# An encoder layer in split float32: the normalised input starts at 64 modulo 256 bytes, and its plain products run in two halves of 256 tokens

## Chip, cores and metric

One core of one Trainium2 chip runs the whole kernel. The metric is device time in microseconds (us), lower is better; three runs were timed.

## The reference

Input `x` is 512 tokens by 1024 features, float32. One layer is computed, and a final RMS norm:

```python
x = x + 0.5 * swiglu(rms_norm(x, ffn1_norm), ffn1_gate, ffn1_up, ffn1_down)   # 1024 -> 2816 -> 1024
x = x + hybrid_mixer(rms_norm(x, mix_norm), w_in, ...)    # w_in 1024 x 3088, w_out 1024 x 1024
x = x + 0.5 * swiglu(rms_norm(x, ffn2_norm), ffn2_gate, ffn2_up, ffn2_down)
return rms_norm(x, final_norm)

def swiglu(h, w_gate, w_up, w_down):
    return (jax.nn.silu(h @ w_gate) * (h @ w_up)) @ w_down
```

The mixer projects the normalised input with `w_in` into the queries, keys, values and gates of a gated linear attention (4 heads, chunks of 64), of a differential attention (4 heads, blocks of 128 queries) and of a short convolution, runs the three, joins their outputs and multiplies them by `w_out`.

## The kernel before

**Precision and layout.** Activations lie transposed in SBUF: features on the 128 partitions, 512 tokens along the free axis, 8 tiles of features. Every large product is made of three matmuls (`three`, lines 519 to 523): each operand is split into a high and a low part in `F32R`, and high x high, high x low and low x high are added up in PSUM. ScalarE makes the high part (`split_hi`, line 1033, for weights), VectorE the low one (`split_lo`, line 1409). `xg_hi` and `xg_lo` hold the normalised input's two parts (before the division by the root mean square, which is applied to the outputs).

**Addresses.** `sb(name, shape)` gives out SBUF in order; tensors opened on one nested stack share memory with those of the next stack. Behind `xg_hi` and `xg_lo` (16384 bytes each on a partition) come `w_hi` and `w_lo` (9216 each), then a region that holds `h` (45056) and, behind a pad of 48 floats (192 bytes), `s_hi` and `s_lo`. Sizes but the pads are multiples of 256. `sum_hi` and `sum_lo` lie behind one more pad of 64 bytes, so that they, the weights' parts `w_hi`, `w_lo`, `h` and `h_hi` start at the same place modulo 256 as `xg` does. Each slice that a matmul takes of `xg` or `s` begins a multiple of 1024 bytes from its tensor's start.

**Order of work.** Up and gate products of FFN 1, its down product, the mixer (27 slabs of `w_in`), `w_out`, then FFN 2 the same way as FFN 1. A slab is 8 blocks of 128 x 128 weights; SP loads it into one of two slots of `raw`, ScalarE and VectorE split it into one of two slots of `w_hi`, `w_lo`, and TensorE waits for it (`wait_slab`).

- *Plain tiles.* The first `PLAIN` = 4 of the 22 tiles of an FFN's hidden features are computed plainly, a gate and an up product each (`pair`, `product`): 8 blocks, three matmuls of 512 columns per block, with `xg` streamed. The very first pair (`first_pair`) does both products block by block while the data arrive.
- *Fast units.* The other `FAST` = 18 tiles use Winograd's form of Strassen's scheme on 2 x 2 blocks: seven block products in place of eight. A unit has 84 matmuls of 256 columns. m1, its companion and m4 stream halves of `xg` (`x_block`; 36 matmuls); m3, m5, m6 and m7 stream sums of activations `s_hi`, `s_lo` (`s_block`; 48). The weights' sums are made by GpSimd (`sums`, lines 445 to 456), split by ScalarE (`ga`, `gb`, line 1152) and VectorE (lines 1465, 1470, 1475) into `sum_hi`, `sum_lo`. ScalarE copies partial results out of PSUM into `snap` (`take`, line 1128), VectorE combines them: lines 1520, 1488, 1525, 1494, 1502 and 1482 (`c11`, `c21`, scaling, `c12`, `gated`, `c22`). ScalarE's own order in a unit is `snap[2]`, `gb`, `split_hi`, `snap[0]`, SiLU of the unit before (line 1134, after line 1488), the `sum_hi` of line 1152, `snap[1]`, `ga`. TensorE's m7 waits for `snap[1]` (lines 663 to 665); VectorE's line 1482 waits for `snap[2]`, which is m7's result.
- *Mixer.* The list `MIX` has 18 transposed tiles ("T": weights loaded, `xg` streamed, 512 columns) and 9 slabs of natural tiles ("N": `xg` loaded as the stationary operand, `w_hi`, `w_lo` streamed, 384 columns). Between the work of a slab, twice per slab, `side(hook(j, half))` puts in the small matmuls of attention and of the recurrence.
- *Last tile.* The last output tile of FFN 2 (`last_tile`) is done in two halves of 256 tokens, with its weights split into the memory of `xg` (`last_hi`, `last_lo`).

Of the kernel before, what the change touches and what calls it, by code (L numbers as in the profile page):

```python
# [29 lines left out]
P = 128  # L30
# [3 lines left out]
KT = D // P  # L34
# [56 lines left out]
def hook(j, half):  # L91
    return 2 * j + half
# [35 lines left out]
def half_tokens(c):  # L128
    return slice(c * HALF, (c + 1) * HALF)
# [25 lines left out]
def build_layer(nc, xT, up_w, down_w, t_w, nat_w, out_w, gains, gk_up, gk_bias, gla_gain, diff_gain,  # L155
                lam_qk, rel_bias, conv_w, onehot, decay_mats, level_masks, ident_c, out):
    tvec = nc.dram_tensor("bias_by_distance", (HEADS * COPIES, 5 * P), F32, kind="Internal")
    with ExitStack() as ctx:
        def sb(name, shape, dt=F32, stack=ctx):
            return stack.enter_context(nc.sbuf_tensor(name, shape, dt))  # L160
# [2 lines left out]
            return ctx.enter_context(nc.semaphore(name))  # L163


        xg_hi = sb("xg_hi", [P, KT, S], F32R)
        xg_lo = sb("xg_lo", [P, KT, S], F32R)
        w_hi = sb("w_hi", [P, 2, SLOTW], F32R)
        w_lo = sb("w_lo", [P, 2, SLOTW], F32R)

# [81 lines left out]
        ps = ctx.enter_context(nc.psum_tensor("ps", [P, 8, S], F32))  # L252
# [262 lines left out]
        def _(pe):  # L515
            def wait_slab(s, n=0):
                pe.wait_ge(lo_ready, n + (s + 1))
# [7 lines left out]
            def part(s, lo, hi):  # L525
                return w_hi[:, slot(s), lo:hi], w_lo[:, slot(s), lo:hi]
# [24 lines left out]
            def spread_rms(phase):  # L551

                pe.wait_ge(diag_ready, phase + 1)
                for b in range(NB):
                    last = pe.matmul(ps[:, STAT, b * P:(b + 1) * P], ones[:], rinv[:, b * P:(b + 1) * P],
                                     start=True, stop=True)
                last.then_inc(stat_ready, 1)
# [15 lines left out]
                        if k == KT - 1:  # L573
                            last.then_inc(slab_used, 1)

            def product(s, bank, first_use, n=0, spread_at=None):
                wait_slab(s, n)
                for k in range(KT):
                    if k == spread_at:
                        spread_rms(0)  # L580
                    if first_use is not None:
                        pe.wait_ge(xg_lo_ready, first_use + k + 1)
                    last = three(ps[:, bank, :], part(s, k * P, (k + 1) * P), (xg_hi[:, k, :], xg_lo[:, k, :]),
                                 k == 0, k == KT - 1)
                return last

            def ffn_up(f, up0):
                phase = 2 * f

                def pair(m):  # L590
                    b = m % 2
                    first = m == 0
                    if m + f >= 2:
                        pe.wait_ge(gate_scaled, PLAIN * f + m - 1)
                        pe.wait_ge(h_ready, FT * f + m - 1)
                    g = up0 + 2 * m
                    last = product(g, b, KT * phase if first else None)
                    last.then_inc(slab_used, 1)
                    second = m == 1 and phase == 0
                    if second or (first and phase):  # L600
                        mean_squares(phase)
                    last = product(g + 1, 2 + b, None, spread_at=KT // 2 if second else None)
                    last.then_inc(slab_used, 1)
                    if first:
                        spread_rms(phase)
# [346 lines left out]
            for j, kind in enumerate(MIX):  # L952
# [4 lines left out]
                if kind[0] == "T":  # L957
# [2 lines left out]
                        pe.wait_ge(tile_copied, t - 1)  # L960
                    if n_nat:
                        pe.wait_ge(nat_copied, NB * (n_nat - 1) + t % 2 + 1)
                    for k in range(KT):
                        last = three(ps[:, t % 2, :], part(s, k * P, (k + 1) * P), (xg_hi[:, k, :], xg_lo[:, k, :]),
                                     k == 0, k == KT - 1)
                        if k == KT // 2 - 1:
                            side(hook(j, 0))
                    last.then_inc(slab_used, 1)

                else:  # L970
                    _, sec, k0, nk = kind
# [1064 lines left out]
```

## Time and profile before

| what | value |
|---|---|
| median of 3 runs | 989.5 us (989.37 to 989.78) |
| profiled execution, own time | 989.01 us |
| its span, first to last instruction | 987.2 us |
| mean granted TensorE clock | 0.994 |
| TensorE busy | 964.1 us (98%) |
| VectorE busy | 682.4 us (69%) |
| ScalarE busy | 437.7 us (44%) |
| GpSimd busy | 353.2 us (36%) |
| read from HBM | 92.00 MB |

The profile is of one execution. A matmul's record covers more than the time in which it keeps the next one back, so the rate is read from starts and not from durations. A clock of 1.00 is the full one. In the rows, PE is TensorE, DVE is VectorE, ACT is ScalarE, POOL is GpSimd; `ps<-a,b` is a matmul with `a` streamed and `b` loaded; square brackets at the end of a row give the idle time of the engine before it and what released it.

### The profile page before, as it was taken

The numbers are of one execution on the slowest core, as the hardware profiler recorded it, in microseconds if no ns is written. First come the engines' busy times: TensorE is split into PE (matmuls) and PEld (weight loads), VectorE is DVE, ScalarE is ACT, GpSimd is POOL, SyncE is SP. The second block draws the span as 40 slices with busy tenths as digits, with TensorE's granted clock in tenths as the row PEclk, the third lists the DMA queues.
The fourth block names the chain that finished last, engine by engine and source line by source line (L and its number), as shares of the span: only waits on it lengthen the run. The fifth ranks groups of instructions, "written<-read, shape, count | busy, mean of one in ns | idle before, by whom it ended". The sixth has DMA issues, their size and how long they took to land.

```text
span 987.2 us, 16662 instructions
## 1 busy us (share of the span) xinstructions
PE 964.1 (98%) x6362; PEld 859.4 (87%) x6362; DVE 682.4 (69%) x948; ACT 437.7 (44%) x687; POOL 353.2 (36%) x229
## 2 busy tenths in 40 slices
PE   9999999999999999999989999999999999999997
PEld 7789999998888888777978788888999999888887
DVE  6599999987534364775756874459999999753444
ACT  7555454555422223555723233355545454542331
POOL 0766767670012151000102004367776767000001
PEclk9999999999999999999979999999999999999999
DMA  6323232322222244112211123233333332222322
GB/s 203 135 81 117 94 124 88 127 85 93 90 87 96 96 133 135 65 47 66 74 39 65 55 74 107 85 107 107 105 109 110 102 115 97 64 96 96 97 96 86
DMA packets 30639, 95.07 MB, mean 96 GB/s; under 512 B 4113, under 2 KB 7345, under 8 KB 30593
## 3 DMA queue, kind: packets, MB, share of 16 engines
q1 hardware_dynamic: 29264, 91.77, 28.4%
q0 software_dynamic: 896, 2.39, 0.8%
q8 instruction: 31, 0.51, 0.2%
q10 hardware_dynamic: 432, 0.28, 0.1%
q14 instruction: 16, 0.12, 0.0%
HBM read 92.00 MB, written 2.42 MB: 96 GB/s over the span
## 4 chain that ended last, share of the span: by engine, by line
PE 42%; DVE 5%; ACT 2%; issue 1%; POOL 0%; DVEq 0%; POOLq 0%; ACTq 0%
PE ps L521 13%; PE ps L523 13%; PE ps L522 13%; ACT w_hi L1033 1%; DVE w_lo L1409 1%; DVE s_lo L1460 1%; DVE e_dec L1742 1%; PE ps L861 1%; DVE a_comp L1762 1%; ACT h L1041 0%; PE ps L893 0%; PE ps L901 0%; PE ps L831 0%; DVE states L1788 0%; DVE h_lo L1556 0%
## 5 line engine op out<-in xcount | busy, mean ns | idle before, releaser
L1409 DVE TENSOR_TENSOR w_lo<-raw,w_hi 128x1024 fp32r<-128x1024 f32 (+3 forms) x130 | 191.6, 1474 | 167.4 <-ACT w_hi L1033 167.3
L1033 ACT ACTIVATE w_hi<-raw 128x1024 fp32r<-128x1024 f32 (+3 forms) x130 | 134.2, 1032 | 209.2 <-PE ps L523 208.7
L521 PE MATMUL ps<-xg_hi,w_hi 128*128 128x256 f32 (+1 forms) x552 | 188.1, 341 | 4.0 <-DVE w_lo L1409 2.4
L523 PE MATMUL ps<-xg_hi,w_lo 128*128 128x256 f32 (+1 forms) x552 | 184.4, 334 | 0.0
L522 PE MATMUL ps<-xg_lo,w_hi 128*128 128x256 f32 (+1 forms) x552 | 184.2, 334 | 0.0
L521 PE MATMUL ps<-s_hi,sum_hi 128*128 128x256 f32 x576 | 159.7, 277 | 1.8 <-ACT snap L1128 1.7
L522 PE MATMUL ps<-s_lo,sum_hi 128*128 128x256 f32 x576 | 159.3, 276 | 0.0
L523 PE MATMUL ps<-s_hi,sum_lo 128*128 128x256 f32 x576 | 159.1, 276 | 0.0
L522 PE MATMUL ps<-h_lo,w_hi 128*128 128x512 f32 x330 | 128.4, 389 | 0.0
L521 PEld LDWEIGHTS ps<-xg_hi,w_hi 128*128 128x128 f32 x552 | 104.4, 189 | 24.1 <-issue 13.4
L523 PEld LDWEIGHTS ps<-xg_hi,w_lo 128*128 128x128 f32 x552 | 104.4, 189 | 10.8
L522 PEld LDWEIGHTS ps<-xg_lo,w_hi 128*128 128x128 f32 x552 | 104.5, 189 | 9.3
L521 PEld LDWEIGHTS ps<-s_hi,sum_hi 128*128 128x128 f32 x576 | 108.3, 188 | 2.5 <-issue 2.5
L522 PEld LDWEIGHTS ps<-s_lo,sum_hi 128*128 128x128 f32 x576 | 108.3, 188 | 0.0
L523 PEld LDWEIGHTS ps<-s_hi,sum_lo 128*128 128x128 f32 x576 | 108.2, 188 | 0.0
L521 PE MATMUL ps<-h_hi_s,w_hi 128*128 128x512 f32 x240 | 93.6, 390 | 0.6 <-DVE h_lo L1556 0.6
L523 PE MATMUL ps<-h_hi_s,w_lo 128*128 128x512 f32 x240 | 93.4, 389 | 0.0
L445 POOL TENSOR_TENSOR t_raw<-raw,raw_u 128x512 f32<-128x512 f32 x36 | 56.0, 1554 | 84.6 <-DMA raw_u<-up_w 74.8
L449 POOL TENSOR_TENSOR t_raw<-raw_u 128x512 f32<-128x512 f32 x36 | 76.4, 2122 | 0.0
L456 POOL TENSOR_TENSOR raw_u<-t_raw,raw 128x512 f32<-128x512 f32 x36 | 70.3, 1953 | 14.4 <-DVE w_lo L1409 7.1
L1134 ACT ACTIVATE gate_s<-gate_s 128x512 f32<-128x512 f32 x34 | 21.5, 634 | 117.6 <-DVE gate_s L1488 117.6
L522 PEld LDWEIGHTS ps<-h_lo,w_hi 128*128 128x128 f32 x330 | 62.0, 188 | 12.5
(243 smaller groups left out, 1901.2 us busy)
## 6 DMA issues: line engine op xcount, KB each, us to landing
raw<-up_w SPq DMA_DIRECT2D x50, 512.0 KB, 4.2
raw<-down_w SPq DMA_DIRECT2D x38, 512.0 KB, 3.3
raw_u<-up_w SPq DMA_DIRECT2D x36, 512.0 KB, 3.3
raw<-t_w SPq DMA_DIRECT2D x18, 512.0 KB, 3.2
raw<-out_w SPq DMA_DIRECT2D x8, 512.0 KB, 3.3
raw<-nat_w SPq DMA_DIRECT2D x6, 576.0 KB, 3.9
x<-xT SPq DMA_DIRECT2D x8, 256.0 KB, 5.3
out<-x SPq DMA_DIRECT2D x8, 256.0 KB, 2.2
```

The lines of the kernel that those rows point to most:

```text
L445: pool.tensor_tensor(t_raw[:, T1, :], raw[:, slot(s), 0:HW], raw_u[:, b, 0:HW], ALU.add)\
L449: pool.tensor_tensor(t_raw[:, T3, :], raw_u[:, b, 0:HW], raw_u[:, b, HW:UPW], ALU.add)\
L456: pool.tensor_tensor(raw_u[:, b, 0:HW], t_raw[:, T2, :], raw[:, slot(s), HW:UPW], ALU.add)\
L521: pe.matmul(out_ap, a[0], b[0], start=first, stop=False, skip_group_check=resumed)
L522: pe.matmul(out_ap, a[0], b[1], start=False, stop=False, skip_group_check=resumed)
L523: return pe.matmul(out_ap, a[1], b[0], start=False, stop=last, skip_group_check=resumed)
L861: last = pe.matmul(ps[c * CHUNK:(c + 1) * CHUNK, bank + hd, col + b * CHUNK:col + (b + 1) * CHUNK], a, bb, start=True, stop=True)
L1033: act.activation(dst, raw[:, slot(s), 0:w], ACT.Copy).then_inc(hi_ready, 1)
L1134: act.activation(gate_s[:, b, :], gate_s[:, b, :], ACT.Silu).then_inc(silu_done, 1)
L1409: dve.tensor_tensor(lo, raw[:, slot(s), 0:w], hi, ALU.subtract).then_inc(lo_ready, 1)
L1460: dve.tensor_tensor(s_lo[:, j, :, :], s_raw[:, j, :, :], s_hi[:, j, :, :], ALU.subtract)\
L1742: dve.tensor_tensor(e, e, g, ALU.mult).then_inc(products_ready, 1)
```

## The change

Two pads, of 192 bytes below `xg_hi` and of 320 above `xg_lo`, move `xg` by 192 bytes and everything behind it by 512. The plain products and the transposed tiles of the mixer are computed in two halves of 256 tokens, all eight blocks for the first half and then all eight for the second; what stood between the fourth and the fifth block (`spread_rms`, the hook) stands between the halves. The gate product of FFN 2's first pair, `first_pair` and the natural tiles keep their shape.

```diff
--- before.py
+++ after.py
@@ -163,8 +163,10 @@
             return ctx.enter_context(nc.semaphore(name))
 
 
+        sb("below_xg", [P, 48])
         xg_hi = sb("xg_hi", [P, KT, S], F32R)
         xg_lo = sb("xg_lo", [P, KT, S], F32R)
+        sb("above_xg", [P, 80])
         w_hi = sb("w_hi", [P, 2, SLOTW], F32R)
         w_lo = sb("w_lo", [P, 2, SLOTW], F32R)
 
@@ -573,15 +575,24 @@
                         if k == KT - 1:
                             last.then_inc(slab_used, 1)
 
-            def product(s, bank, first_use, n=0, spread_at=None):
-                wait_slab(s, n)
+            def product(s, bank, first_use):
+                wait_slab(s)
                 for k in range(KT):
-                    if k == spread_at:
-                        spread_rms(0)
-                    if first_use is not None:
-                        pe.wait_ge(xg_lo_ready, first_use + k + 1)
+                    pe.wait_ge(xg_lo_ready, first_use + k + 1)
                     last = three(ps[:, bank, :], part(s, k * P, (k + 1) * P), (xg_hi[:, k, :], xg_lo[:, k, :]),
                                  k == 0, k == KT - 1)
+                return last
+
+            def product_by_halves(s, bank, between):
+
+                wait_slab(s)
+                for c in range(2):
+                    t = half_tokens(c)
+                    for k in range(KT):
+                        last = three(ps[:, bank, t], part(s, k * P, (k + 1) * P), (xg_hi[:, k, t], xg_lo[:, k, t]),
+                                     k == 0, k == KT - 1)
+                    if c == 0 and between is not None:
+                        between()
                 return last
 
             def ffn_up(f, up0):
@@ -594,12 +605,15 @@
                         pe.wait_ge(gate_scaled, PLAIN * f + m - 1)
                         pe.wait_ge(h_ready, FT * f + m - 1)
                     g = up0 + 2 * m
-                    last = product(g, b, KT * phase if first else None)
+                    if first:
+                        last = product(g, b, KT * phase)
+                    else:
+                        last = product_by_halves(g, b, None)
                     last.then_inc(slab_used, 1)
                     second = m == 1 and phase == 0
                     if second or (first and phase):
                         mean_squares(phase)
-                    last = product(g + 1, 2 + b, None, spread_at=KT // 2 if second else None)
+                    last = product_by_halves(g + 1, 2 + b, (lambda: spread_rms(0)) if second else None)
                     last.then_inc(slab_used, 1)
                     if first:
                         spread_rms(phase)
@@ -960,12 +974,7 @@
                         pe.wait_ge(tile_copied, t - 1)
                     if n_nat:
                         pe.wait_ge(nat_copied, NB * (n_nat - 1) + t % 2 + 1)
-                    for k in range(KT):
-                        last = three(ps[:, t % 2, :], part(s, k * P, (k + 1) * P), (xg_hi[:, k, :], xg_lo[:, k, :]),
-                                     k == 0, k == KT - 1)
-                        if k == KT // 2 - 1:
-                            side(hook(j, 0))
-                    last.then_inc(slab_used, 1)
+                    product_by_halves(s, t % 2, lambda: side(hook(j, 0))).then_inc(slab_used, 1)
 
                 else:
                     _, sec, k0, nk = kind
```

## Rows read from the trace of the kernel before

**Rows 1.** the page, busy time, share of the span and instructions of each engine
```profile
PE 964.1 (98%) x6362; PEld 859.4 (87%) x6362; DVE 682.4 (69%) x948; ACT 437.7 (44%) x687; POOL 353.2 (36%) x229
```

**Rows 2.** TensorE's groups by shape: line, streamed and loaded operand, count; busy, mean ns
```profile
L521 PE MATMUL ps<-s_hi,sum_hi 128*128 128x256 f32 x576 | 159.7, 277 | 1.8 <-ACT snap L1128 1.7
...
L521 PE MATMUL ps<-xg_hi,w_hi 128*128 128x512 f32 x264 | 106.6, 404 | 1.9 <-ACT dv L1360 0.8 <-issue 0.7 <-DVE w_lo L1409 0.3
...
L521 PE MATMUL ps<-xg_hi,w_hi 128*128 128x256 f32 x288 | 81.5, 283 | 2.1 <-DVE w_lo L1409 2.1
...
L521 PE MATMUL ps<-xg_hi,sum_hi 128*128 128x256 f32 x144 | 40.9, 284 | 1.1 <-ACT snap L1128 1.1
...
L521 PE MATMUL ps<-w_hi,xg_hi 128*128 128x384 f32 x96 | 33.4, 348 | 0.0
...
L522 PE MATMUL ps<-h_lo,xg_hi 128*128 128x256 f32 x44 | 12.4, 283 | 0.0
```

**Rows 3.** timeline of TensorE, one steady unit: start us, duration us
```profile
752.71 0.28 PE L521 MATMUL ps<-xg_hi,w_hi 128*128 128x256 f32 x1
...
757.01 0.29 PE L521 MATMUL ps<-s_hi,sum_hi 128*128 128x256 f32 x1
...
761.11 0.28 PE L521 MATMUL ps<-s_hi,sum_hi 128*128 128x256 f32 x1
...
762.47 0.28 PE L521 MATMUL ps<-xg_hi,w_hi 128*128 128x256 f32 x1
```

**Rows 4.** ten steady units: window, busy us (instructions) of each engine, granted clock, DMA
```profile
713.67:811.27 97.60, 97.60 (x843) 97.60 (x841) 91.20 (x101) 50.65 (x80) 70.97 (x41) 1.00 0.33 107
```

**Rows 5.** timeline of TensorE, 512 columns: steady, and behind a hook
```profile
20.12 0.39 PE L523 MATMUL ps<-xg_hi,w_lo 128*128 128x512 f32 x1
...
20.80 0.39 PE L523 MATMUL ps<-xg_hi,w_lo 128*128 128x512 f32 x1
...
430.54 0.50 PE L521 MATMUL ps<-xg_hi,w_hi 128*128 128x512 f32 x1
...
433.39 0.27 PE L796 MATMUL ps<-ident,u 128*128 128x128 f32 x1
```

**Rows 6.** timeline of VectorE, steady units
```profile
734.17 0.41 DVE L1482 SCALAR_TENSOR_TENSOR h<-ps,snap 128x256 f32 x1
...
753.54 0.43 DVE L1482 SCALAR_TENSOR_TENSOR h<-ps,snap 128x256 f32 x1
...
755.62 2.32 DVE L1409 TENSOR_TENSOR w_lo<-raw,w_hi 128x1024 fp32r<-128x1024 f32 x1
...
758.20 0.41 DVE L1488 TENSOR_TENSOR gate_s<-ps,rinv 128x256 f32<-128x256 f32 x1
...
760.32 1.30 DVE L1475 TENSOR_TENSOR sum_lo<-raw_u,sum_hi 128x1024 fp32r<-128x1024 f32 x1 [0.61 <-ACT sum_hi L1152]
...
763.24 0.41 DVE L1482 SCALAR_TENSOR_TENSOR h<-ps,snap 128x256 f32 x1
```

**Rows 7.** timeline of ScalarE in the same unit
```profile
758.70 0.63 ACT L1134 ACTIVATE gate_s<-gate_s 128x512 f32<-128x512 f32 x1 [3.59 <-DVE gate_s L1488]
...
760.18 0.36 ACT L1128 ACTIVATE snap<-ps 128x256 f32<-128x256 f32 x1
```

**Rows 8.** timeline of TensorE, m7 of the third unit of FFN 1
```profile
84.27 0.36 PE L521 MATMUL ps<-s_hi,sum_hi 128*128 128x256 f32 x1 [0.99 <-ACT snap L1128]
```

**Rows 9.** timeline of GpSimd in the unit of rows 6
```profile
755.50 1.35 POOL L445 TENSOR_TENSOR t_raw<-raw,raw_u 128x512 f32<-128x512 f32 x1 [2.44 <-DMA raw_u<-up_w]
```

**Rows 10.** timeline of VectorE in two late units of FFN 1
```profile
205.69 1.21 DVE L1409 TENSOR_TENSOR w_lo<-raw,w_hi 128x1024 fp32r<-128x1024 f32 x1
...
208.82 0.42 DVE L1494 SCALAR_TENSOR_TENSOR h<-ps,snap 128x256 f32 x1 [0.49 <-PE ps L523]
...
215.51 1.21 DVE L1409 TENSOR_TENSOR w_lo<-raw,w_hi 128x1024 fp32r<-128x1024 f32 x1
```

**Rows 11.** VectorE writing s_lo: count, ns min/median/max, first and last start
```profile
L1460 DVE TENSOR_TENSOR s_lo<-h,s_hi x8: 1212/2310/2318, 46.4 to 671.9; 128x1024 fp32r<-128x1024 f32 x8
```

## The prediction

> **What bounds the kernel now.** I read the page first: TensorE is busy for 98% of the span [rows 1]. Then the groups of matmuls by shape, which give the counts [rows 2]. The durations there hold a tail that overlaps the next matmul, so the price of a matmul is the distance between two starts, read from TensorE's timeline. In one unit of the fast loop, the 36 matmuls that stream `xg` start at 752.71 and end where `s` takes over at 757.01: 4.30 us, 119.4 ns each (120 once settled). The last 12 that stream `s`, 761.11 to 762.47, take 113.3 ns each [rows 3]. Both are 256 columns against weights of the same kind, at the full granted clock, 2.4 GHz [rows 4], where 256 columns alone are 106.7 ns. With `xg` it is 120 in the groups against `w` and against `sum` alike, 283 ns in duration where `s` has 277 [rows 2]. What differs is the start: between `xg` and `s` the allocations are multiples of 256 bytes, but for a pad of 192, so `s` lies at 64 modulo 256 and `xg` at 128. With 512 columns at 128, three matmuls take 0.68 us, 226.7 ns each, against 213.3 of columns alone [rows 5]. So at 128 a matmul carries 13.3 ns on top whatever its width, and at 64, with 256 columns, 6.7.
>
> Then VectorE's timeline of the same unit, since it is busy for 91.2 of 97.6 us there [rows 4]. This decides the forecast. Its cycle, from one `h` of line 1482 to the next, is 9.70 us (753.54 to 763.24) with no wait for TensorE in it, against TensorE's 9.76 (752.71 to 762.47) [rows 3, 6]. Its one idle spell, 0.61 us before line 1475, is a wait for ScalarE, and ScalarE had waited for VectorE's line 1488 [rows 6, 7]. The chain is closed: 1488 at 758.20, SiLU at 758.70, `sum_hi`, then the copy of `snap` at 760.18 that ends at 760.54, and `sum_lo`. TensorE's product m7 needs that `snap` and starts at 761.11, 0.57 us after it [rows 3]. At 84.27, where the steady part of the first fast loop begins, m7 started right behind `snap` after 0.99 us of idle time [rows 8]; the same shows at 702.45 for the second FFN. So both loops start with TensorE waiting for VectorE, and the lead VectorE then gains is small.
>
> **The change, part by part.**
>
> *The offset.* `xg_hi` and `xg_lo` move to 64 modulo 256; all else keeps its place modulo 256. A unit's 36 `xg` matmuls fall from 4.30 to 36 x 0.1133 = 4.08 us, and the `s` part loses some 0.02 of settling, so TensorE's own unit falls by 0.24, from 9.76 to 84 x 0.1133 = 9.52. With TensorE alone, 36 units would give 8.6 us. But VectorE's cycle is 9.70, of which TensorE's speed changes nothing: the lengths that stretch it come from GpSimd's work (line 1409 takes 2.32 us while GpSimd's line 445 runs [rows 6, 9], and 1.21 where VectorE came first [rows 10]). From the anchor at 84.27 to m7 of the last unit are 15 units: 15 x (9.76 - 9.69) = 1.05 us, with 9.69 the mean of the three free cycles from 734.17 to 763.24 [rows 6]. Some cycles differ: VectorE starts line 1409 just before GpSimd, ends it 1.1 us sooner, and then waits 0.49 us for TensorE at line 1494; from 205.69 to 215.51 is 9.82 with that wait [rows 10]. I count five such cycles in the 30. A faster TensorE takes the wait away, which leaves 9.33, 0.36 under the free cycle, though some of it comes back as contention. Half of 2.5 x 0.36 is 0.4, rounded down to 0.35. That makes 1.4 us for each loop, **2.8** for both. Bounds: 0.5 for each if VectorE's cycle only eats the end's slack, 15 x 0.24 = 3.6 if it doesn't bind at all; so 1.0 to 7.2. The units before the anchors give nothing, as TensorE idles behind ScalarE and VectorE there.
>
> *The halves.* Of the 768 matmuls of 512 columns in plain products (six in the first FFN after the first pair, eight in the second) and in 18 transposed tiles, 24 each, the gate product of the second FFN's first pair stays whole. That leaves 744, which become 1488 of 256 columns with their weights loaded twice. 1488 x 113.3 = 168.6 us against 744 x 226.7 = 168.7: **0**. This rests on the price of `s` holding for `xg` against `w_hi` and `w_lo`. Those lie where `sum_hi` and `sum_lo` lie modulo 256, and today `xg` costs 120 against both, which speaks for it. If they cost 120 after all, the halves cost 744 x 13.3 = 9.9 us more; that is a rival. Loading 256 columns' weights keeps pace in the `s` parts. Line by line, the work between the halves (attention, transposes, scores) stands where it stood, halfway through a tile, and no wait is added. The consumers wait for the tile's last matmul, as before.
>
> The Trainium skill (TensorE: Matmul & The Clock Gate, Back-to-back issue gap) gives N / 2.4 + 2.5 ns, which is 109.2 ns for 256 columns wherever the operand lies. By it the offset would save nothing and each split would cost 2.5 ns, 1.9 us in all. The trace shows two prices for one width, so here it does not hold as it stands.
>
> *The settling after a hook.* After the small matmuls between halves, 12 matmuls of 512 columns take 2.85 us (430.54 to 433.39) against 2.72 in a steady run [rows 5]: 0.13 more. The first weight load after the hook stays exposed; with 256 columns I take 0.015 less for the settling behind it. With two such places in each of 18 tiles, 36 x 0.015 = **0.5** us gained; bounds 0 and 36 x 0.13 = 4.7, the low end being the nearer.
>
> *512 columns at 64.* The first pair of slabs (48 matmuls) and the gate product above (24) stay whole with `xg` at 64, for which no row exists. Below: 213.3 + 6.7 = 220.0, 72 x 6.7 = 0.5 us gained. Above: the extra doubles to 26.7, 72 x 13.3 = 1.0 lost. I take **0**.
>
> *`xg` as the stationary operand.* In the natural tiles (96 x 3 = 288 matmuls of 384 columns [rows 2]) `xg` is what is loaded, and in the last output tile (44 x 3 = 132 of 256 columns [rows 2]) weights lie in its memory. If what counts is the distance between the two operands, each gains or loses 6.7 ns: 1.9 and 0.9 us, either way. If only the streamed operand counts, nothing. I take **0**; the natural tiles' share is partly behind waits anyway.
>
> *ScalarE, VectorE, DMA.* They write and read `xg` at 64 now. No cost: VectorE writes `s_lo` at 64 in 1.21 us at best [rows 11], the 1.21 of `w_lo` at 128 [rows 10].  Instruction count rises by 744 matmuls and their loads on TensorE's queue; the straight-line last tile already runs 256-column matmuls without gaps.
>
> Sum: 2.8 + 0 + 0.5 + 0 + 0 = 3.3 us. The profiled execution took 989.0 us (span 987.2 and 1.8 around it); 989.0 - 3.3 = 985.7. The median of the runs is 0.5 above it, which gives **986.2**.
>
> **Rivals.**
>
> 1. VectorE gives way, TensorE keeps its 9.52. For it: the cycles of [rows 10], where VectorE waits; GpSimd was ahead of line 1409 by only 0.12 us (755.50 against 755.62 [rows 6, 9]), so the order may flip for good once VectorE never waits for TensorE. Against: in the free cycles it does not flip, and total contention per unit is much the same. 7.2 + 0.5 = 7.7 saved: 981.8. Chance 0.20.
>
> 2. Hidden or given back: the loops gain only 2.0 and the unpriced operands (512 at 64, `xg` loaded from 64) take it back: 2.0 - 1.0 - 1.0 = 0, so 989.5. For it: none of the three has a row. Chance 0.17.
>
> 3. Slower: the address is not what makes `s` cheaper. Then all splits pay the fixed 13.3 ns twice, 9.9 us, and nothing is gained: 999. It decides from 3.3 / 1488 = 2.2 ns more for each half matmul than 113.3. For it: no 256-column `xg` matmul at 64 is in the trace. Against: equal shapes, weights and clock in [rows 3]. Chance 0.08, a milder form included, in which the halves reach 116 to 118 and the loops gain nothing (4 to 7 us, 993 to 997). The Trainium skill's formula, above, would be another mild form, at 1.9 us.
>
> The forecast, VectorE's cycle setting the loops at 9.6 to 9.7, 984 to 988, has 0.55.
>
> **How the numbers follow.** This kernel's measurement tells about 0.2% (2 us) from no change, so faster means under 987.5. The forecast gives that in 0.8 of its cases (0.44), rival 1 always (0.20), rival 2 rarely (0.03): 0.67. Slower than 991.5: rival 3 and a small part of rival 2, 0.10. The rest, 0.23, lies between. The range reaches down past rival 1 with a little of the loaded operand's gain, 980.5, and up to rival 2 with 0.3 on top, 989.8; outside are the slower cases and a few lucky ones. The forecast's own range is 984 to 988.
>
> **What would show it.** In the profile after: starts of `xg` matmuls of 256 columns 113.3 ns apart in units, plain products and tiles (1, 3); the unit's length, 9.6 to 9.7 for me, 9.52 for rival 1, 9.76 for rival 3; idle time of TensorE before m7, released by ScalarE's `snap`, some 0.1 to 0.2 us in each unit, and no waits of VectorE at line 1494; the starts in the natural tiles (173.3 now) and in the last tile (120 now); the first pair's distance (226.7 now). I am wrong if VectorE's cycle falls below 9.5, if halves don't reach 113.3, or if 512 columns at 64 cost far more than the bounds.

## The result: slower by 0.36%

The changed kernel takes 993.2 us (median of 6 executions, 992.26 to 995.18) against 989.64 of the kernel before (6, 988.66 to 990.69): ratio 1.0036, 95% interval 1.0025 to 1.0046. I had forecast 986.2, with 980.5 to 989.8 as the range; the time is 3.4 us above that range. Line numbers differ between the kernels: in rows of the changed kernel and its variants the matmul helper is L523 to L525 (L521 to L523 before), `w_lo` L1418 (L1409), `snap` L1137 (L1128), and `c22`, the last write of `h` in a unit, L1491 (L1482).

The page of the changed kernel, busy time of the engines, answers to [rows 1]. TensorE has 744 more matmuls and is busy 4.4 us longer; the other engines' counts are as they were.

```profile
PE 968.5 (98%) x7106; PEld 896.5 (91%) x7106; DVE 684.3 (69%) x948; ACT 436.6 (44%) x687; POOL 357.8 (36%) x229
```

TensorE's groups by shape, against [rows 2]. I had read the gap between 277 (`s`) and 283 (`xg`) as two prices, and expected `xg` to come down to `s`. Both groups now stand at 281: `s`, which the change does not touch, came up.

```profile
L523 PE MATMUL ps<-s_hi,sum_hi 128*128 128x256 f32 x576 | 161.9, 281 | 1.8 <-ACT snap L1137 1.8
...
L523 PE MATMUL ps<-xg_hi,sum_hi 128*128 128x256 f32 x144 | 40.5, 281 | 1.1 <-ACT snap L1137 1.1
```

TensorE's timeline of one steady unit, against [rows 3] (start, duration):

```profile
745.10 0.28 PE L523 MATMUL ps<-xg_hi,w_hi 128*128 128x256 f32 x1
...
749.34 0.28 PE L523 MATMUL ps<-s_hi,sum_hi 128*128 128x256 f32 x1
...
753.58 0.28 PE L523 MATMUL ps<-s_hi,sum_hi 128*128 128x256 f32 x1
...
754.99 0.28 PE L523 MATMUL ps<-xg_hi,w_hi 128*128 128x256 f32 x1
```

The 36 `xg` matmuls take 4.24 us, 117.8 ns each, and the last 12 of `s` 1.41, 117.5 by these rounded starts. The unit is 9.89 us (84 x 117.8) where it was 9.76 and I wanted 9.52 to 9.69. From m7 of the third unit to m7 of the last, the first FFN's loop grew by 1.75 us and the second's by 1.53. These two make 3.28 us, and the whole span grew by 3.25 (987.22 to 990.47). The rest cancels. The first pair starts 0.74 us sooner, and the plain products of the second FFN gain 0.67. The transposed tiles up to the attention lose 0.50. One tile (541.29) loses 1.34 to the clock; of the fifteen profiles of this study nine have this tile slow and six have not, kernels with whole and with split products among either. The windows of that tile in the changed kernel and in the one before; the third number from the end is the granted clock (0.65 against 1.00, so that part of it ran at the 1.2 GHz level):

```profile
541.29:545.50 4.21, 4.21 (x26) 4.21 (x25) 2.70 (x4) 0.00 (x0) 0.00 (x0) 0.65 0.01 4
```

```profile
539.91:542.78 2.87, 2.87 (x16) 2.31 (x13) 2.63 (x4) 0.00 (x0) 0.00 (x0) 1.00 0.00 0
```

**Where 117.8 comes from.** 117.8 is not a fixed price: in the same trace, the steady part of the first loop starts at 113.3. TensorE's timeline around m7 of its fourth unit:

```profile
93.18 0.28 PE L523 MATMUL ps<-s_hi,sum_hi 128*128 128x256 f32 x1
93.30 0.28 PE L524 MATMUL ps<-s_lo,sum_hi 128*128 128x256 f32 x1
93.41 0.28 PE L525 MATMUL ps<-s_hi,sum_lo 128*128 128x256 f32 x1
93.56 0.36 PE L523 MATMUL ps<-s_hi,sum_hi 128*128 128x256 f32 x1
93.75 0.28 PE L524 MATMUL ps<-s_lo,sum_hi 128*128 128x256 f32 x1
93.87 0.28 PE L525 MATMUL ps<-s_hi,sum_lo 128*128 128x256 f32 x1
```

ScalarE's timeline at that moment, the copy that m7 waits for; it ends at 93.41:

```profile
93.05 0.36 ACT L1137 ACTIVATE snap<-ps 128x256 f32<-128x256 f32 x1
```

Up to 93.41 the starts are 113 or 114 ns apart. TensorE, with its 9.52 us of work, has caught up with `snap`; m7 starts 146 ns after its predecessor and has 193 ns behind it. From 93.75 on the starts are 117 to 119 ns apart, for 1185 matmuls, to 233 us. In the second FFN the same stop at 723.63 (193 ns) ends the fast stretch, and 1101 matmuls at 117.8 follow. Not every stop does this: the one at 713.99, with 148 and 195 ns, left 113.3 in place. At 9.89 the unit is longer than VectorE's cycle, so TensorE never stops again and nothing brings it back. VectorE's timeline shows who waits now, against [rows 6]: the cycle from `w_lo` to `w_lo` is 9.81 and 9.98 in turn, TensorE's 9.89 in the mean, and holds a wait of 0.20 for `snap` that [rows 6] don't have.

```profile
738.11 2.31 DVE L1418 TENSOR_TENSOR w_lo<-raw,w_hi 128x1024 fp32r<-128x1024 f32 x1
...
747.92 2.31 DVE L1418 TENSOR_TENSOR w_lo<-raw,w_hi 128x1024 fp32r<-128x1024 f32 x1
...
755.82 0.42 DVE L1491 SCALAR_TENSOR_TENSOR h<-ps,snap 128x256 f32 x1 [0.20 <-ACT snap L1137]
...
757.90 2.31 DVE L1418 TENSOR_TENSOR w_lo<-raw,w_hi 128x1024 fp32r<-128x1024 f32 x1
```

So my theory (**two steady distances**): 256 columns streamed from 64 modulo 256 run at 113.3 or at 117.8 ns; which of them is settled when TensorE starts again after a stop, and it stays until the next stop, or until operands from another start have passed. In the kernel before, each unit's 36 matmuls from 128 were such an interruption, and `s` was at 113.3 behind every one of them. The rivals: a fixed price of this order of instructions, and contention with VectorE.

### The profile page after: what moved, and what is told of

The parts are those of the page before. It is cut to its first block and busy times, and to the rows that moved or that the text cites. A ratio compares the mean times of both kernels' runs of the same rounds, so it can differ in the third digit from the quotient of the medians.

```text
span 990.5 us, 18166 instructions
## 1 busy us (share of the span) xinstructions
PE 968.5 (98%) x7106; PEld 896.5 (91%) x7106; DVE 684.3 (69%) x948; ACT 436.6 (44%) x687; POOL 357.8 (36%) x229
## 5 line engine op out<-in xcount | busy, mean ns | idle before, releaser
L1418 DVE TENSOR_TENSOR w_lo<-raw,w_hi 128x1024 fp32r<-128x1024 f32 (+3 forms) x130 | 197.2, 1517 | 167.1 <-ACT w_hi L1042 167.0
L523 PE MATMUL ps<-xg_hi,w_hi 128*128 128x256 f32 (+1 forms) x800 | 229.3, 287 | 3.0 <-DVE w_lo L1418 1.6
L525 PE MATMUL ps<-xg_hi,w_lo 128*128 128x256 f32 (+1 forms) x800 | 225.5, 282 | 0.0
L524 PE MATMUL ps<-xg_lo,w_hi 128*128 128x256 f32 (+1 forms) x800 | 225.4, 282 | 0.0
L523 PE MATMUL ps<-s_hi,sum_hi 128*128 128x256 f32 x576 | 161.9, 281 | 1.8 <-ACT snap L1137 1.8
L523 PEld LDWEIGHTS ps<-xg_hi,w_hi 128*128 128x128 f32 x800 | 151.2, 189 | 13.4 <-issue 11.4
L525 PE MATMUL ps<-s_hi,sum_lo 128*128 128x256 f32 x576 | 161.5, 280 | 0.0
L525 PEld LDWEIGHTS ps<-xg_hi,w_lo 128*128 128x128 f32 x800 | 152.0, 190 | 0.7
L524 PEld LDWEIGHTS ps<-xg_lo,w_hi 128*128 128x128 f32 x800 | 151.0, 189 | 0.7
L523 PEld LDWEIGHTS ps<-s_hi,sum_hi 128*128 128x128 f32 x576 | 108.2, 188 | 2.5 <-issue 2.4
L525 PEld LDWEIGHTS ps<-s_hi,sum_lo 128*128 128x128 f32 x576 | 110.2, 191 | 0.0
L523 PE MATMUL ps<-h_hi_s,w_hi 128*128 128x512 f32 x240 | 93.6, 390 | 0.6 <-DVE h_lo L1565 0.6
L525 PE MATMUL ps<-h_hi_s,w_lo 128*128 128x512 f32 x240 | 93.4, 389 | 0.0
L451 POOL TENSOR_TENSOR t_raw<-raw_u 128x512 f32<-128x512 f32 x36 | 80.3, 2231 | 0.0
```

Source lines behind the costliest of these rows:

```text
L451: pool.tensor_tensor(t_raw[:, T3, :], raw_u[:, b, 0:HW], raw_u[:, b, HW:UPW], ALU.add)\
L523: pe.matmul(out_ap, a[0], b[0], start=first, stop=False, skip_group_check=resumed)
L524: pe.matmul(out_ap, a[0], b[1], start=False, stop=False, skip_group_check=resumed)
L525: return pe.matmul(out_ap, a[1], b[0], start=False, stop=last, skip_group_check=resumed)
L1418: dve.tensor_tensor(lo, raw[:, slot(s), 0:w], hi, ALU.subtract).then_inc(lo_ready, 1)
```

## The experiments

All on kernels of the same reference; ratios are to the kernel before, run on the same chip. Where no ratio is given, one execution was timed. "Unit" is the distance of two starts of `xg` against `sum_hi` in a steady part of a loop.

**1 and 2. One part of the change at a time.** `offset_only` has the two pads and the old whole products:

```diff
+        sb("below_xg", [P, 48])
         xg_hi = sb("xg_hi", [P, KT, S], F32R)
         xg_lo = sb("xg_lo", [P, KT, S], F32R)
+        sb("above_xg", [P, 80])
```

`halves_only` has `product_by_halves` and no pads.

> The pads alone: xg at 64, plain products and transposed tiles whole, 512 columns. Theory L (a matmul of 256 columns that streams from 64 has two steady distances, 113.3 and 117.8 ns; which one holds is fixed when TensorE restarts after a stop, and the blocks at 128 used to reset it in every unit): the fast loops sit at 117.8 in most units as in the changed kernel, 9.89 us a unit, and the 512-column matmuls take 232 to 234 ns as in the changed kernel's first pair, 6 to 7 ns over 226.7, so 744 of them cost some 5 us over the kernel before; with some 3 from the loops, 996 to 998. Rival S (the halves' doubled instructions and loads slow TensorE down, not the offset): loops at 113.3 and some 986 to 988.

> The halves alone: xg stays at 128. Theory L: 256 columns at 128 take 120 ns, 240 for a pair against 226.7, 744 x 13.3 = 9.9 us more, little of it hidden: 998 to 1000; the fast units stay at 9.76. Rival S: the same direction, but the fast units would slow down too, beyond 1000.

Measured: `offset_only` 994.13 us (10 executions, 989.21 to 995.70), ratio 1.0034 (1.0018 to 1.0050). Its units are 9.89 in both loops; 113.3 is lost in the first at a short stop before m7 again (136 and 192 ns, at 93.2), in the second at a stop of 1.24 us before the third unit's m7. Its 512 columns cost 233. `halves_only` 994.78 (993.47 to 997.13), ratio 1.0046 (1.0032 to 1.0059). Its units are 9.76 throughout, its halves 120, and 24 of them behind a hook take 2.98 us against 2.85 for the 12 whole ones of [rows 5]. So each part alone loses about as much as both together: the offset loses in the loops and in 512 columns, the halves lose at 128 and no longer at 64. It also shows that the loss in the loops is the offset's alone. `offset_only` stayed below its 996 to 998. One of its executions took 989.21 while the others took 992 to 996, perhaps a first sign that the price isn't fixed. `halves_only` fell short of its 998 to 1000; only part of the 9.9 us is in its profile (span +6.2).

**3. One matmul from 128 at each unit's start.** Would it act as the interruption that the kernel before had?

```diff
+                    if not isinstance(i, int):
+                        pe.wait_ge(start_dve, 2)
+                        for _ in range(1):
+                            pe.matmul(ps[:, 7, 0:HALF], g_hi[:, 0:P], g_hi[:, 0:HALF], start=True, stop=True)
```

> The changed kernel with one matmul of 256 columns more at the start of each unit inside the two fast loops, streamed and loaded from the weights' high part, which lies at 128 modulo 256; its result is not used. Theory L: a stream from 128 resets the distance, so the unit's 84 matmuls go back to 113.3 (9.52 us) and with the extra one to 9.64, bounded by VectorE's own cycle of 9.7; against 9.89 now some 0.2 us in each of 30 units, 986 to 989. If one such matmul is too short to reset it, 0.12 x 32 = 4 us are added: 997. Rival T (117.8 comes from other traffic at that time, DMA or the other engines): nothing is reset, 997.

Measured: 993.18 (10, 991.25 to 1000.12), ratio 1.0035 (1.0012 to 1.0058). It doesn't act so: the second loop ran at 117.8 to its end, though every unit had the extra matmul (units 10.01). The first loop, in the same profile, held 113.3 from 77 to 213 us, units of 9.66 to 9.76, through two short stops (145 and 126 ns), and fell to 117.8 behind a third (162 ns at 212.8). One program, the same instructions in both loops, two distances. The wait added a stop of 3.2 us to the first unit, so the total says little.

**4 and 5. Only one of the two operands at 64** (halves as in the changed kernel). `lo_at_64` moves `xg_lo` alone, `hi_at_64` `xg_hi` alone:

```diff
-        sb("below_xg", [P, 48])
         xg_hi = sb("xg_hi", [P, KT, S], F32R)
+        sb("between_xg", [P, 48])
         xg_lo = sb("xg_lo", [P, KT, S], F32R)
-        sb("above_xg", [P, 80])
+        sb("above_xg", [P, 16])
```

`hi_at_64` keeps the pad below `xg_hi` and puts 16 floats between the two and 64 above.

> The changed kernel with xg_hi at 128 and only xg_lo at 64 (pads of 192 bytes between the two and 64 behind). Theory L, if each matmul pays for its own start: two of three matmuls in a block at 120, the third at 113.3, mean 117.8, and s at 113.3 throughout since xg_hi resets it. If the distance belongs to the pair of neighbours, another mean, between 113.3 and 120. Time some 993 to 996.

> As the changed kernel, with xg_hi at 64 modulo 256 and xg_lo back at 128, so two of each three matmuls of an xg product stream from 64 and one from 128. Theory, the address sets the price and a row of matmuls from 128 puts the distance from 64 back to 113.3 ns: s at 113.3 in every unit of both loops, xg at (2 x 113.3 + 120) / 3 = 115.5 or, if a matmul from 64 right behind one from 128 does not come down, up to 118; TensorE alone would need 36 x 115.5 + 48 x 113.3 = 9.60 us for a unit, VectorE's 9.69 then binds, m7 waits some 0.1 us for snap; both loops some 1 us shorter than before, T tiles and halves 2 to 3 us dearer by the split: 989 to 991. Rival, the distance is set only by how TensorE restarts after a stop: loops at 117.8 and 9.89 again, 993 or more.

Measured: 991.06 and 992.07 (one execution each), 2 us below the first's forecast and 1 above the second's. TensorE's timeline of a unit of `lo_at_64`:

```profile
739.10 0.28 PE L523 MATMUL ps<-xg_hi,sum_hi 128*128 128x256 f32 x1
...
740.51 0.28 PE L523 MATMUL ps<-s_hi,sum_hi 128*128 128x256 f32 x1
...
745.97 0.28 PE L523 MATMUL ps<-xg_hi,w_hi 128*128 128x256 f32 x1
...
748.79 0.28 PE L523 MATMUL ps<-xg_hi,sum_hi 128*128 128x256 f32 x1
```

`s` takes 745.97 - 740.51 = 5.46 us for 48, 113.8 with two or three settling matmuls, the same in every unit without a stop; `xg` averages (1.41 + 2.82) / 36 = 117.5 by these rounded starts, near the plain mean of 120, 120 and 113.3, which is 117.8, and the unit is 9.69. In the steady units of `hi_at_64` `s` is at 113.3 too, `xg` averages 119.2 (the plain mean is 115.5, so switching between starts cost nearly as much here as staying at 128), and the unit is 9.73.

That streams from 128 put `s` back at 113.3 shows best where a stop has just left it at 117.8. TensorE's timeline of `halves_only`, with all of `xg` at 128: eleven distances behind a stop, 718.57 to 719.86, are 117 each; behind the next 36 from 128, `s` takes 729.63 - 724.17 = 5.46 us for 48, 113.8 each.

```profile
718.57 0.28 PE L522 MATMUL ps<-s_lo,sum_hi 128*128 128x256 f32 x1
...
719.86 0.28 PE L521 MATMUL ps<-xg_hi,w_hi 128*128 128x256 f32 x1
...
724.17 0.29 PE L521 MATMUL ps<-s_hi,sum_hi 128*128 128x256 f32 x1
...
729.63 0.28 PE L521 MATMUL ps<-xg_hi,w_hi 128*128 128x256 f32 x1
```

The profiles hold eight such places without another stop between, in kernels in which all 36 or 24 of the 36 stream from 128, and `s` came back in all eight. With 12 of 36 from 128 (`hi_at_64`) it came back once and once not.

**6 and 7. Other offsets.** Pads of 32 and 96 floats put `xg` at 0, of 16 and 112 at 192.

```diff
-        sb("below_xg", [P, 48])
+        sb("below_xg", [P, 32])
...
-        sb("above_xg", [P, 80])
+        sb("above_xg", [P, 96])
```

> As the changed kernel, with xg at 0 modulo 256 instead of 64 (pads of 128 and 384 bytes). Weights stay at 128 and s at 64. If the start of the streamed operand within 256 bytes is what counts and a stream from a multiple of 256 is the best case: xg at 113.3 or below in every stretch, 512 columns at 220 to 226.7, units at VectorE's 9.69, 986 to 988. If it is whether the streamed and the loaded operand start at the same place modulo 256 (both at 128 before): 113.3 or 117.8 for each stretch as at 64, 990 to 996. If 0 and 128 are alike (the start counts modulo 128): xg at 120, loops 9.76 as before, halves 744 x 13.3 = 9.9 us less what the restarts save, so 994 to 999.

> As the changed kernel, with xg at 192 modulo 256 (pads of 64 and 448 bytes). Weights stay at 128 and s at 64. If the start counts modulo 128, 192 is like 64: 113.3 or 117.8 by stretch, 512 columns at 232 to 234, the time within 989 to 995 as in the changed kernel. If the distance to the loaded operand counts, 192 is 64 above the weights where 64 is 64 below, a case without a row: between 113.3 and 120. Either way s follows 36 matmuls that stream from elsewhere; if a switch of the start is what puts s back to 113.3, s shows 113.3 in every unit, and if it takes streams from 128, s stays at the distance of the stretch before.

Measured: 991.99 and 992.53. At 0, `xg` averages 119 with starts 115 to 122 apart; in steady units `s` is at 113.3 and the unit is 9.73. But in the second loop a stop of 366 ns left `s` at 117.8, and 36 streams from 0 did not bring it back: a whole unit (9.93) and the next up to its m7 stayed there, until another stop. At 192, `xg` is at 117.8. In the steady part of the first loop `s` was at 113.3 and the unit at 9.69. In the second loop the second unit's `s` was at 113.3 until a stop before m7, and at 117.8 from there to the end, with units of 9.89. TensorE's timeline: 35 distances up to 693.43 in 3.97 us, 113.4 each, the stop, and the next unit's `s`, 5.65 us for 48, 117.7 each:

```profile
689.46 0.28 PE L523 MATMUL ps<-s_hi,sum_hi 128*128 128x256 f32 x1
...
693.43 0.28 PE L525 MATMUL ps<-s_hi,sum_lo 128*128 128x256 f32 x1
693.82 0.36 PE L523 MATMUL ps<-s_hi,sum_hi 128*128 128x256 f32 x1
...
699.55 0.28 PE L523 MATMUL ps<-s_hi,sum_hi 128*128 128x256 f32 x1
...
705.20 0.28 PE L523 MATMUL ps<-xg_hi,w_hi 128*128 128x256 f32 x1
```

In this profile 36 streams from 192 followed `s` at 117.8 nineteen times; twice it came back, 17 times not. So not every change of the start puts `s` back, and none of four offsets is better for `xg` than 64 at its fast distance. The weights, which are what is loaded, stayed at 128 in all of these kernels, so the start of the streamed operand and its distance from the loaded one's are not told apart. With 512 columns the kernel before has the best place: 226.7 at 128, 229 at 192, 230 to 235 at 0, and 233 at 64.

**8. The changed kernel once more.**

> The changed kernel once more, for a second profile. My theory: 256 columns from 64 run at one of two steady distances, 113.3 or 117.8 ns, fixed where TensorE starts again after a stop and kept until the next. Then each loop shows one of the two from its start to its end, units of 9.69 (VectorE's cycle) or 9.89 us, with nothing between, and the loops together make 989 (both at 113.3) to 993 or more (both at 117.8); which of them it is may differ from the first profile. Rival, the distance is a fixed price of this order of instructions: both loops at 9.89 again, to 0.01 us, and the span within 0.3 us of the first profile's.

Measured: 993.41, span 991.6, both loops at 9.89 in the end. The first lost 113.3 at the same short stop before m7 (176 and 193 ns, at 93.3). The second lost it at a long one, before the fourth unit's m7, behind which the starts are 117 to 119 ns apart:

```profile
713.83 0.28 PE L525 MATMUL ps<-s_hi,sum_lo 128*128 128x256 f32 x1
715.08 0.36 PE L523 MATMUL ps<-s_hi,sum_hi 128*128 128x256 f32 x1 [0.97 <-ACT snap L1137]
```

So my "one of the two from its start to its end" did not hold, since both loops switched on the way; the rival's span within 0.3 us of the first profile's didn't either (1.1 longer). The time alone speaks as much for a fixed price, so the next ones were made.

**9, 10 and 11. VectorE never late.** In the loops' units VectorE makes only half, or a quarter, of `w_lo`; the rest of the tile keeps what an earlier slab left there.

```diff
-            def split_lo(s, n=0):
+            def split_lo(s, n=0, share=1):
...
-                w = slab_width(s)
+                w = slab_width(s) // share
...
-                        split_lo(s + 1, 2 * i)
+                        split_lo(s + 1, 2 * i, 2)
```

> The changed kernel, but in the loop's units with a following one VectorE makes only the first half of w_lo (the rest keeps what an earlier slab left there, so the output is not the reference's). VectorE's cycle falls by about half of 2.3 us, to some 8.6 us, under TensorE's 9.52. Theory, two steady distances, chosen where TensorE starts again after a stop, and the fast one was lost in both profiles because at 113.3 TensorE needs 9.52 and catches up with VectorE's 9.69, stops before m7, and comes back at 117.8: without that stop a loop that starts at 113.3 keeps it to its end, all units at 9.52, and the first loop, which began at 113.3 at 84 us in both profiles, ends 3.5 us or more sooner than with the full split; a loop that starts at 117.8 stays at 9.89. Rival, the distance drifts to 117.8 by itself or is set by the order of matmuls: 9.89 in both loops, though VectorE is never late. Second rival, contention with VectorE is what keeps 117.8: then lighter work gives units between 9.52 and 9.89.

> As the run with half of w_lo, with a quarter of it, so VectorE's cycle is some 8.0 us. By the theory of two steady distances the units take 9.52 or 9.89 with nothing between, each loop as it started, and VectorE's load changes neither figure. By contention the units would be shorter than with half. If both loops show 9.89 in both kernels, the fast distance is not lost by the stop but cannot be kept by whole units of this order, and my theory falls.

> The changed kernel with half of w_lo left out in the loops' units, the same program as before, now timed in several executions. Theory: each of the two loops falls on 113.3 or 117.8 where it starts and keeps it, 15 to 17 units x 0.37 = 5.6 to 6.3 us apart, so the times lie near 981 (both fast), 986 to 987 (one of them) and 992 (both slow), with little between. Rival, the distance follows from the program: the times agree to 0.5%, all at 981, and the run with a quarter of w_lo at 992 is another program with another order in time.

Measured: half of `w_lo`, 980.74; a quarter, 992.33; half again, 986.16 as the median of five, which are 985.15, 985.42, 986.16, 991.17 and 991.26. TensorE's timeline of the first, the first loop's first steady unit and 14 units on:

```profile
87.77 0.28 PE L523 MATMUL ps<-xg_hi,sum_hi 128*128 128x256 f32 x1
...
221.05 0.28 PE L523 MATMUL ps<-xg_hi,sum_hi 128*128 128x256 f32 x1
```

The same of the second execution profiled, of the same program, with its entry into the loop:

```profile
82.92 0.35 PE L523 MATMUL ps<-s_hi,sum_hi 128*128 128x256 f32 x1 [0.21 <-ACT snap L1137]
...
87.23 0.28 PE L523 MATMUL ps<-xg_hi,sum_hi 128*128 128x256 f32 x1
...
225.74 0.28 PE L523 MATMUL ps<-xg_hi,sum_hi 128*128 128x256 f32 x1
```

And the kernel with a quarter of `w_lo`:

```profile
87.40 0.28 PE L523 MATMUL ps<-xg_hi,sum_hi 128*128 128x256 f32 x1
...
225.91 0.28 PE L523 MATMUL ps<-xg_hi,sum_hi 128*128 128x256 f32 x1
```

133.28 / 14 = 9.52 us in the one, 138.51 / 14 = 9.89 in the other two, with nothing between, and the second loops agree with the first in each of the three. One program gave both, on two chips; on the second chip alone its times fall into two groups. The two distances are therefore not a matter of the instructions, nor of VectorE's load: less load gave the same 9.89, and one load gave both. With no stop in a loop, whichever it had at the entry lasted to the end, some 1270 matmuls. The second loop of the profile of 980.74 had one stop inside, 301 ns between two starts, and was back at 113.3 behind it; so a stop need not cost the fast distance:

```profile
707.33 0.28 PE L525 MATMUL ps<-s_hi,sum_lo 128*128 128x256 f32 x1
707.63 0.36 PE L523 MATMUL ps<-s_hi,sum_hi 128*128 128x256 f32 x1
```

The five times and the 980.74 lie in three groups, near 981, 985.6 and 991.2, as both loops fast, one of the two, and none would make them; of the middle group no execution was profiled, so that reading of it is argued.

**12. The control.** The same half of `w_lo` left out of the kernel before.

> The kernel before with the same half of w_lo left out in the loops' units. It separates what the lighter VectorE gives from what the address gives. Theory: TensorE sets 9.76 there (36 x 120 + 48 x 113.3), so the units stay at 9.76; only the stops of the first units shrink by 1 to 2 us over both loops: 987 to 989, ratio 0.998 to 1.000. Against 980.7 of the changed kernel with the same edit that leaves 30 units x 0.24 = 7.2 us for the address at its fast distance. Rival, the lighter VectorE itself gave most of the 980.7: 981 to 984.

Measured: 987.27 (10, 986.48 to 988.37), ratio 0.9980 (0.9971 to 0.9990). Its unit is 9.76, from 96.78 to 223.66 for 13, and the 1.8 us come from the stops of the first units. So with VectorE out of the way the offset and the halves give 987.27 - 980.74 = 6.5 us where both loops are fast and cost 3.9 where both are slow (991.2). The 980.74 is a single execution on another chip; taken against the kernel before on its own chip (989.83 there, 989.08 here) the gain is 9.1 - 1.8 = 7.3 us, and 30 x 0.24 = 7.2 was expected. Over all executions there is no gain to be seen: the changed kernel with half of `w_lo` has the ratio 0.9979 (0.9955 to 1.0004) over five, the kernel before with the same edit 0.9980.

**13. Can the sure part of it be had?** Whole products, and `xg_lo` at 64 in the two FFN phases only:

```diff
-        xg_lo = sb("xg_lo", [P, KT, S], F32R)
+        xg_lo_mem = sb("xg_lo", [P, KT * S + 64], F32R)
+        xg_lo_ffn, xg_lo_mix = (xg_lo_mem[:, c:c + KT * S].rearrange("p (k s) -> p k s", s=S) for c in (48, 0))
```

> The kernel before (whole products of 512 tokens) with one thing changed: in the two FFN phases xg_lo is written and read 192 bytes further on, at 64 modulo 256, in the mixer it stays at 128; xg_hi is at 128 throughout. Theory: from the look at halves with xg_lo alone at 64, the xg matmuls of a loop unit average 117.8 and s is back at 113.3 in each unit, so a unit is 36 x 117.8 + 48 x 113.3 = 9.68, or VectorE's 9.69, against 9.76: 30 x 0.07 = 2.1 us gained. The 512 column matmuls of the FFN products cost 229 against 226.7: 384 x 2.3 = 0.9 us lost. Net 1.2 us gained, ratio 0.9988, so 988 to 989; the mixer's steps unchanged. Rival, the loops start on VectorE anyway and eat the gain up, or the 512 columns cost 233 as with both at 64 (2.5 us): 989.5 to 991.

Measured: 989.15 (12, 988.54 to 992.84) against 989.83, ratio 0.9999 (0.9990 to 1.0009): no difference. Units are 9.69, which is VectorE's cycle, with some of 9.73 to 9.85 where TensorE stops for it; the loops gain 0.81 and 0.53 us of the 2.1, and the 512 columns (229 in place of 226.7) take part of it back. No version here that computes the whole result beats the kernel before.

## Why the prediction was wrong

**The price of a matmul from 64, the step that failed.** "The price of `s` holding for `xg`" was right as far as it goes: `xg` at 64 does run at 113.3, in the fourth unit of the changed kernel, and in both loops of experiment 9 (980.74) to their ends. What failed is that I took 113.3 for a property of the address. It is one of two, 4.5 ns apart, and [rows 3] could not show the other, since there each unit's `xg` part, at 128, stands between two `s` parts. The trace of before did hold it, in one place. Its timeline of TensorE where the second unit's last `s` part begins behind a stop:

```profile
71.46 0.28 PE L523 MATMUL ps<-s_hi,sum_lo 128*128 128x256 f32 x1
71.75 0.36 PE L521 MATMUL ps<-s_hi,sum_hi 128*128 128x256 f32 x1
71.95 0.28 PE L522 MATMUL ps<-s_lo,sum_hi 128*128 128x256 f32 x1
...
73.12 0.28 PE L523 MATMUL ps<-s_hi,sum_lo 128*128 128x256 f32 x1
```

From 71.95 to 73.12 are ten distances, 117 each, with `s` at 64 and no `xg` near. I read only steady units and passed it over. The change then took out the interruption that kept such stretches short. With 117.8 TensorE's own unit is 84 x 117.8 = 9.89 in place of 9.52, 0.13 above the old one; over two loops 30 x 0.13 = 3.9 us, of which 3.28 show.

**VectorE's cycle sets the loops (2.8 us).** Right for as long as TensorE is at 113.3: while `xg` and `s` ran at 113.3, m7 stopped briefly for `snap`, as foreseen, and such a unit of the changed kernel, from 708.66 to 718.30, took 9.64. But I counted the stops as harmless. They are the moments at which 113.3 can be lost: a VectorE at 9.69 makes TensorE at 9.52 stop in each unit, and a TensorE at 9.89 never stops. The slow distance lasts once it is reached. In the three profiles of whole `xg` at 64 and full `w_lo`, all six loops ended in it: four lost 113.3 at a short stop before m7, as TensorE caught up with VectorE's cycle, and two (the second loops of `offset_only` and of the repeat) at a stop of 1.24 or 1.25 us in the loop's first units, where the kernel before has one of about a microsecond too [rows 8]. The gain of 2.8 became a loss of 3.3.

**Rival 1 (9.52, VectorE gives way).** Not here; experiment 9 shows TensorE's 9.52 once VectorE has less to do. **Rival 3.** The time fell into the range of its milder form, 993 to 997, but by another way: it put the loss in the halves and none in the loops, and here the halves cost next to nothing and the loops lost 3.3. I gave all of it 0.08, and it was to decide from 2.2 ns more for each half matmul than 113.3; in the loops' matmuls it came to 4.5. Its ground, that the address is not what makes `s` cheaper, is only half true: at 128 a steady run costs 120, at 64 one of two lower prices. **Rival 2** had the wrong sign for the loops.

**The halves (0).** About right at 64: 48 of them take 5.45 us (113.5 each) from 18.50 in the changed kernel and 5.66 (117.9) in its repeat, since each stretch settles anew. A tile of 24 behind a hook takes 2.85 or 2.93, against 2.85 to 2.90 before, so the **settling (0.5)** is not to be seen either. `halves_only` shows what they cost at 128.

**512 columns at 64 (bounds 220 to 240).** 233, on the dear side: 72 x 6.6 = 0.5 us lost in place of 0. TensorE's timeline, three matmuls in 0.69 or 0.70 us, where [rows 5] has 0.68:

```profile
11.51 0.39 PE L523 MATMUL ps<-xg_hi,first_hi 128*128 128x512 f32 x1
...
12.20 0.40 PE L523 MATMUL ps<-xg_hi,w_hi 128*128 128x512 f32 x1
...
12.90 0.39 PE L523 MATMUL ps<-xg_hi,first_hi 128*128 128x512 f32 x1
```

**`xg` as the loaded operand (0).** Natural tiles: 173.3 before and after. The last tile, whose streamed `h` stays where it was modulo 256: 120 before, 117.8 after, 132 x 2.2 = 0.3 us gained. So what is loaded counts a little. **Writes at 64**: no cost, as forecast (`w_lo` 2.31 against 2.32).

**The skill's rule.** The Trainium skill (TensorE: Matmul & The Clock Gate, Back-to-back issue gap) gives one gap for a width, 109.2 ns for 256 columns as an estimate; it calls this the gap of an isolated matmul, too low at small widths where each matmul has its own weight load and too high at large ones. The traces have 113.3, 117.8 and 120 for that width at full clock, all above it, and for 512 columns 226.7 or more, also above the formula's 215.8, so it does not hold here as it stands, and 1.9 us for the splits is not what they cost at either address.

**What stays open.** Why there are two distances, and why a given restart falls on one or the other. The length of the stop alone does not decide: behind 145, 148 and 301 ns 113.3 stayed, behind 136, 146 and 162 it went. The moment of the restart may decide it; no run here sets that moment, nor varies GpSimd's work or the DMA traffic, which one program has alike in its executions at either distance. That a row of 36 matmuls, 24 or more of them from 128, puts `s` back is shown by `halves_only` and the seven places like it; that a single one doesn't, by experiment 3; how many it takes is not. Whether 128 does this by its place or by being where the weights start is open too.

## What to carry to other kernels

A price taken from a steady stretch is that of the stretch: before moving work to another address, look in the trace for all distances that the same shape shows, and for what stands between two such stretches. An engine made faster than its supplier stops more often, and if its rate depends on how it restarts, the stops can cost more than the speed gave. Taking the supplier's cycle down removes those stops, but not the ones at a loop's entry: of the six loops profiled so, four were slow from there on. When times of one program fall into groups, look at several executions before the mean is explained.

## What the runs showed of the hardware

- Same instructions, same full granted clock: 256 columns from 64 run at 113.3 or 117.8 ns a matmul, for over 1200 matmuls on end, and one program showed each in different executions (units of 9.52 and 9.89 us).
- A stop of some 20 to 80 ns beyond the normal distance can change it (136 ns in `offset_only`; 146 ns at 93.4 and 193 at 723.6 in the changed kernel); the one at 714.0 (148 ns), and one of 301 ns in experiment 9, did not.
- 36 matmuls of which 24 or all stream from 128 put the next ones from 64 back from 117.8 to 113.3, eight times of eight; from 192 they did so twice in nineteen, from 0 not in two, and a single one from 128 in each unit did not.
- With the weights at 128, the start of the streamed operand modulo 256 bytes and the width count together: 256 columns cost 113.3 or 117.8 at 64, 117.8 at 192, 119 at 0, 120 at 128; 512 columns 233, 229, 230 to 235, and 226.7.
- Two streams from different starts in turn (`xg_hi` at 64, `xg_lo` at 128) average 119.2, though one alone has 113.3 and the other 120.
